# Filling TensorE's waits in the routing stage, and moving two experts' down weights to the end of the load queue

## The reference

```python
h = h + merged @ w_out
u2 = rmsnorm(h, norm_ffn)
p_group = softmax(u2 @ wg + bg)                    # 4 groups, the best one is taken
e_logits = (u2 @ we + be)[chosen group]            # 8 experts in it, the best two are taken
combine = one_hot(group) * g_val * weights_of_the_two
for each of the 32 experts e:                      # 1024 -> 256 -> 1024
    y += (silu(u2 @ w_gate[e]) * (u2 @ w_up[e]) * combine[e]) @ w_down[e]
out = rmsnorm(h + y, norm_final)
```

## Time and profile before

| | us |
|---|---|
| Median of 3 runs | 1137.32 (1136.3 to 1138.05) |
| The profiled execution's own time | 1138.34 |
| Its span, first to last instruction | 1136.5 |
| PE busy in the span | 1040.1 (92%) |
| DVE, ACT, POOL busy | 476.9, 314.8, 59.0 |
| DMA, mean over the span | 153 GB/s |

### The profile page before, as it was taken

How to read it: one execution, slowest core, us unless ns; L and a number is a source line. 1 busy time by engine, 2 the same in 40 slices (tenths; PEclk the granted TensorE clock), 3 DMA queues, 4 the chain that set the end, 5 groups by cost and what they waited for, 6 DMA issues and landing times.

```text
span 1136.5 us, 15499 instructions
## 1 busy us (share of the span) xinstructions
PE 1040.1 (92%) x6445; PEld 630.8 (55%) x6445; DVE 476.9 (42%) x972; ACT 314.8 (28%) x602; POOL 59.0 (5%) x69
## 2 busy tenths in 40 slices
PE   6999999998999999999999999999996999787780
PEld 6665656675575575575566566444454655344440
DVE  4536364637337337337335454523235321111115
ACT  3535344434234334334332122110110111100112
POOL 1000000000000000000000000000001222211110
PEclk9999999999999999999999999999996999988995
DMA  9322222233132132132112111044936999999945
GB/s 287 90 64 66 57 57 56 56 80 73 39 63 72 38 65 70 39 65 70 38 37 75 56 56 57 1 160 165 366 143 240 408 414 416 416 418 414 418 200 231
DMA packets 111946, 174.41 MB, mean 153 GB/s; under 512 B 9012, under 2 KB 87101, under 8 KB 103555
## 3 DMA queue, kind: packets, MB, share of 16 engines
q1 hardware_dynamic: 97890, 130.73, 33.3%
q10 hardware_dynamic: 8256, 31.53, 7.0%
q0 software_dynamic: 5728, 11.14, 3.9%
HBM read 169.16 MB, written 12.60 MB: 160 GB/s over the span
## 4 chain that ended last, share of the span: by engine, by line
PE 68%; DMA 14%; DVE 12%; ACT 3%; issue 2%; SPq 1%; POOL 0%; DVEq 0%; POOLq 0%
PE ps L746 21%; DMA arena<-in_expert_w_up 11%; PE ps L737 7%; PE ps L743 7%; PE ps L744 6%; PE ps L2001 6%; DVE arena L1284 4%; PE ps L1707 3%; PE ps L791 3%; PE ps L2008 2%; PE ps L770 1%; DVE arena L1441 1%; DVE yT L2330 1%; DVE arena L1520 1%; DVE arena L1517 1%
## 5 line engine op out<-in xcount | busy, mean ns | idle before, releaser
L746 PE MATMUL ps<-arena 128*128 128x512 f32 x672 | 314.0, 602 | 0.0
L746 PEld LDWEIGHTS ps<-arena 128*128 128x128 f32 x672 | 119.6, 190 | 113.6 <-issue 108.5
L2001 PE MATMUL ps<-arena,gates 128*64 128x256 f32 x864 | 107.7, 406 | 25.9 <-DMA arena<-in_expert_w_up 24.4
L743 PE MATMUL ps<-arena 128*128 128x264 f32 x416 | 127.9, 389 | 0.8 <-DVE gates L1356 0.8
L744 PE MATMUL ps<-arena 128*128 128x264 f32 x416 | 126.6, 386 | 0.0
L1284 DVE TENSOR_TENSOR arena<-arena 128x256 f32<-128x256 f32 (+6 forms) x194 | 91.5, 516 | 56.5 <-ACT arena L1105 34.3
L2001 PEld LDWEIGHTS ps<-arena,gates 128*64 128x64 f32 x864 | 65.0, 147 | 75.4 <-DMA arena<-in_expert_w_up 35.0
L737 PE MATMUL ps<-yT,arena 128*128 128x512 f32 x192 | 84.8, 596 | 2.2 <-DVE gates L1356 1.4
L744 PEld LDWEIGHTS ps<-arena 128*128 128x128 f32 x416 | 79.0, 190 | 13.5
L743 PEld LDWEIGHTS ps<-arena 128*128 128x128 f32 x416 | 76.0, 190 | 16.3 <-issue 4.7
L2156 DVE COPY gates<-ps 128x1024 f32<-128x1024 f32 x16 | 19.6, 1225 | 110.7 <-PE ps L1988 110.7
(11 more groups left out here) (329 smaller groups left out, 1257.8 us busy)
## 6 DMA issues: line engine op xcount, KB each, us to landing
arena<-in_w_in SPq DMA_DIRECT2D x68, 512.0 KB, 3.8
arena<-in_expert_w_gate SPq DMA_DIRECT2D x27, 1024.0 KB, 28.9
arena<-in_expert_w_up SPq DMA_DIRECT2D x27, 1024.0 KB, 34.6
arena<-in_expert_w_down ACTq DMA_DIRECT2D x18, 1024.0 KB, 32.7
arena<-in_w_branch SPq DMA_DIRECT2D x12, 512.0 KB, 3.9
C<-in_expert_w_gate SPq DMA_DIRECT2D x5, 1024.0 KB, 32.3
gates<-in_expert_w_up SPq DMA_DIRECT2D x5, 1024.0 KB, 38.5
arena<-in_w_out SPq DMA_DIRECT2D x1, 4096.0 KB, 13.8
```

Of the source, the lines that this page charges most:

```text
L743: t.matmul(dst[:, 0:HALF], wt, uT[:, k, 0:HALF], start=(k == 0), stop=(k == KD - 1))
L746: mm = t.matmul(dst, wt, uT[:, k, META:], start=(k == 0), stop=(k == KD - 1))
L2001: mm = t.matmul(dst, toks[:, k, :], src, start=(k == 0), stop=(k == KD - 1))
```

## The change

It has four parts.

1. **Repeated product.** PE gets a function `keep_busy(n)` that makes n products of the identity matrix with 512 columns of the transposed tokens into PSUM bank 5; nobody reads them. It stands 15 times behind the last logits, 2 times behind "ct" and 11 times behind "tb".
2. **Last tile.** The logits of tiles 0 to 2 are scaled ahead of the last copy of the last tile (PE signals them with a new step "l2"), those of tile 3 in one step "l3" from a bank of their own. The last tile is normed ahead of "l3", not behind "num", and ACT stores it ahead of its two exponentials.
3. **Shorter chain.** "O1" and "O2" become one step "O", for which "og" is made twice as wide, and "dm" moves behind "num".
4. **Down weights.** `LATE = 2`: the down weights of experts 30 and 31 are no longer issued by ACT but by SP, behind the last gate and up weights.

```diff
             rows_order = [..., "t2", "u2", "t3a", "h7",
-                          "t3b"]
+                          "sc", "lb", "t3b", "u3"]
...
 scalar:
+                a.wait_ge(*dve2.after(f"u{NT - 1}"))
+                a.dma_start(u2_dram[(NT - 1) * P:, :], u2[:, NT - 1, :]).then_inc(sem("rows_kept"), 16)
                 a.wait_ge(*dve2.after("lt"))
                 a.activation(gx, lt, ACT.Exp).then_inc(*act2.did("eg"))
                 a.wait_ge(*dve2.after("dm"))
                 a.activation(e2, dm, ACT.Exp).then_inc(*act2.did("e2"))
-                a.wait_ge(*dve2.after(f"u{NT - 1}"))
-                a.dma_start(u2_dram[(NT - 1) * P:, :], u2[:, NT - 1, :]).then_inc(sem("rows_kept"), 16)
...
 tensor:
+                def keep_busy(n):
+                    for _ in range(n):
+                        t.matmul(bank(5), ident, u2T[:, KD - 1, :], start=True, stop=True)
...
-                logits(2, every, "t2")
+                logits(2, every, "t2").then_inc(*pe2.did("l2"))
                 turn_tokens(3, high_half, "T3b")
                 logits(3, low_half, "t3a")
                 logits(3, high_half, "t3b").then_inc(*pe2.did("lg"))
+                keep_busy(15)
                 t.wait_ge(*dve2.after("M"))
...
                 mm.then_inc(*pe2.did("ct"))
+                keep_busy(2)
...
                 mm.then_inc(*pe2.did("tb"))
+                keep_busy(11)
...
 vector:
+                first = NT - 1
+                v.wait_ge(*pe2.after("l2"))
+                tt("sc", lg[:, 0:first, :], bank(0, first * 36)..., ss2[:, 0:first]..., ALU.mult)
+                tt("lb", lg[:, 0:first, :], lg[:, 0:first, :], over(rb, first), ALU.add)
                 turned(NT - 1, 1)
+                normed(NT - 1)
                 v.wait_ge(*pe2.after("lg"))
-                v.wait_ge(*act2.after(f"rs{NT - 1}"))
-                tt("sc", lg, bank(0, NT * 36)..., ss2..., ALU.mult)
-                tt("lb", lg, lg, over(rb, NT), ALU.add)
+                step("l3", v.scalar_tensor_tensor(lg[:, first, :], logit_bank(first), ss2[:, first:NT], rb, ALU.mult, ALU.add))
...
-                tt("dm", dm, m2, m1, ALU.subtract)
-                for k, o_ in ((0, o1), (1, o2)):
-                    tt(f"O{k + 1}", chosen[:, k, :]..., og..., o_..., ALU.mult)
+                tt("O", chosen..., og..., o12..., ALU.mult)
                 tt("M", mm_, chosen[:, 0, :], chosen[:, 1, :], ALU.add)
                 tt("num", numbered, by_expert, NUM..., ALU.mult)
-                normed(NT - 1)
+                tt("dm", dm, m2, m1, ALU.subtract)
...
 esync:
                 for e in range(NX - U):
                     sp.wait_ge(*up_made.of(e))
                     load_up(sp, e % U, e + U)
+                for e in range(NX - U - LATE, NX - U):
+                    sp.wait_ge(*made.of(e))
+                    load_down(sp, e % U, e + U)
...
 escalar:
-                    if e + U < NX:
+                    if e + U < NX - LATE:
                         load_down(a, e % U, e + U)
```

More of the change, by code:

```diff
@@ L1622, in tail @@
             nfin = gates[:, 22:24, :].rearrange("p a t -> p (a t)")
-            pe2 = Steps(sem("router_pe"), ["o0", "o1", "o2", "T0", "o3", "o4", "T1", "o5", "o6", "T2", "T3a", "o7", "T3b", "lg",
+            pe2 = Steps(sem("router_pe"), ["o0", "o1", "o2", "T0", "o3", "o4", "T1", "o5", "o6", "T2", "T3a", "o7", "l2", "T3b", "lg",
                                            "rk", "ct", "tb"])
-            choose = ["sc", "lb", "gm", "lt", "gd", "gx", "og", "el", "es", "m1", "e1", "q1", "x1", "o1",
-                      "n2", "m2", "e2", "q2", "x2", "o2", "dm", "O1", "O2", "M", "num", f"u{NT - 1}"]
+            choose = ["l3", "gm", "lt", "gd", "gx", "og", "el", "es", "m1", "e1", "q1", "x1", "o1",
+                      "n2", "m2", "e2", "q2", "x2", "o2", "O", "M", "num", "dm"]
             place = ["rk", "pos", "sl0", "sl1", "vi", "xe", "xo", "yi"]
@@ L1630, in tail @@
                     ["sx", "jb", "jc"], ["jd", "ji", "ni", "eq", "en", "et"], ["vx", "xx", "yx"]]
-            rows_order = ["wn", "h0", "h1", "h2", "t0", "u0", "h3", "h4", "t1", "u1", "h5", "h6", "t2", "u2", "t3a", "h7", "t3b"]
+            rows_order = ["wn", "h0", "h1", "h2", "t0", "u0", "h3", "h4", "t1", "u1", "h5", "h6", "t2", "u2", "t3a", "h7", "sc", "lb", "t3b", "u3"]
             dve2 = Steps(sem("router_dve"), rows_order + choose + place + share + [n for part in more for n in part])
@@ L1681, in scalar, with logit_bank @@
                 a.activation(e2, dm, ACT.Exp).then_inc(*act2.did("e2"))
-                a.wait_ge(*dve2.after(f"u{NT - 1}"))
-                a.dma_start(u2_dram[(NT - 1) * P:, :], u2[:, NT - 1, :]).then_inc(sem("rows_kept"), 16)
+            def logit_bank(i):
+                return bank(0)[:, i * 36:(i + 1) * 36] if i < NT - 1 else bank(1, 36)
             def tensor(t):
@@ L1697, in logits @@
                     for k in ks:
-                        mm = t.matmul(bank(0)[:, i * 36:(i + 1) * 36], u2T[:, k, i * P:(i + 1) * P], wr[:, k, :],
+                        mm = t.matmul(logit_bank(i), u2T[:, k, i * P:(i + 1) * P], wr[:, k, :],
                                       start=(k == 0), stop=(k == KD - 1))
@@ L1746, in tensor @@
                 mm.then_inc(*pe2.did("tb"))
-            lt, gx, og = small(NT, NG), small(NT, NG), small(NT, NG)
+                keep_busy(11)
+            lt, gx, og = small(NT, NG), small(NT, NG), small(2 * NT, NG)
             t4 = small(NT, NG)
             gm, gv, m1, m2, dm, e2, mx = (small(NT) for _ in range(7))
-            el, o1, o2, t8 = small(NT, NE), small(NT, NE), small(NT, NE), small(NT, NE)
+            el, t8, o12 = small(NT, NE), small(NT, NE), small(2 * NT, NE)
+            o1, o2 = o12[:, 0:NT, :], o12[:, NT:, :]
             chosen = small(2, NT * NX)
@@ L1830, in vector @@
                     residual(2 * i + 1)
+                step, tt, ts, red, slots_of = small_steps(v)
+                first = NT - 1
+                v.wait_ge(*pe2.after("l2"))
+                tt("sc", lg[:, 0:first, :], bank(0, first * 36).rearrange("p (i c) -> p i c", i=first),
+                   ss2[:, 0:first].unsqueeze(2).broadcast_to([P, first, 36]), ALU.mult)
+                tt("lb", lg[:, 0:first, :], lg[:, 0:first, :], over(rb, first), ALU.add)
                 turned(NT - 1, 1)
-                step, tt, ts, red, slots_of = small_steps(v)
+                normed(NT - 1)
                 def wide(ap, n):
@@ L1837, in vector @@
                 v.wait_ge(*pe2.after("lg"))
-                v.wait_ge(*act2.after(f"rs{NT - 1}"))
-                tt("sc", lg, bank(0, NT * 36).rearrange("p (i c) -> p i c", i=NT), ss2.unsqueeze(2).broadcast_to([P, NT, 36]), ALU.mult)
-                tt("lb", lg, lg, over(rb, NT), ALU.add)
+                step("l3", v.scalar_tensor_tensor(lg[:, first, :], logit_bank(first), ss2[:, first:NT], rb, ALU.mult, ALU.add))
                 g4, g32 = lg[:, :, 0:NG], lg[:, :, NG:].rearrange("p i (g e) -> p i g e", g=NG)
@@ L1846, in vector @@
                 red("gx", mx, t4, ALU.max)
-                tt("og", og, t4, wide(mx, NG), ALU.is_equal)
-                tt("el", sel, g32, og.unsqueeze(3).broadcast_to([P, NT, NG, NE]), ALU.mult)
+                tt("og", og.rearrange("p (k i) g -> p k i g", k=2), t4.unsqueeze(1).broadcast_to([P, 2, NT, NG]),
+                   mx.unsqueeze(1).unsqueeze(3).broadcast_to([P, 2, NT, NG]), ALU.is_equal)
+                tt("el", sel, g32, og[:, 0:NT, :].unsqueeze(3).broadcast_to([P, NT, NG, NE]), ALU.mult)
                 red("es", el, sel.rearrange("p i g e -> p i e g"), ALU.add)
@@ L1859, in vector @@
                     tt("o" + n, o_, t8, wide(mx, NE), ALU.is_equal)
-                tt("dm", dm, m2, m1, ALU.subtract)
-                for k, o_ in ((0, o1), (1, o2)):
-                    tt(f"O{k + 1}", chosen[:, k, :].rearrange("p (i g e) -> p i g e", i=NT, g=NG),
-                       og.unsqueeze(3).broadcast_to([P, NT, NG, NE]), o_.unsqueeze(2).broadcast_to([P, NT, NG, NE]), ALU.mult)
+                tt("O", chosen.rearrange("p k (i g e) -> p (k i) g e", i=NT, g=NG), og.unsqueeze(3).broadcast_to([P, 2 * NT, NG, NE]),
+                   o12.unsqueeze(2).broadcast_to([P, 2 * NT, NG, NE]), ALU.mult)
                 tt("M", mm_, chosen[:, 0, :], chosen[:, 1, :], ALU.add)
                 tt("num", numbered, by_expert, NUM.unsqueeze(2).broadcast_to([P, 2 * NT, NX]), ALU.mult)
-                normed(NT - 1)
+                tt("dm", dm, m2, m1, ALU.subtract)
                 v.wait_ge(*pe2.after("rk"))
@@ L1896, in tail @@
             WX, WP, PAIR = 3 * 2 * D, 2 * D, 2 * SLOTS
-            U, YR = 6, len(yr)
+            U, YR, LATE = 6, len(yr), 2
             def in_one(at):
```

## The result

The changed kernel took 1143.29 us at the median of 5 runs (1141.23 to 1144.25), beside 1137.32 for the kernel before (5 runs, 1136.3 to 1140.33) in the same comparison. The medians are 6.0 us apart. The ratio, which is formed from all the runs and not from the two medians, is 1.0042, 95% interval 1.0029 to 1.0055: slower by 0.42%, about 4.8 us. The profiled execution took 1141.74, 3.4 more than the 1138.34 of the one profiled before, with a span of 1139.8.

What follows compares the result with a forecast made beforehand. Transfers were taken to bound the expert stage, at 416 GB/s. Its shift of +7.7 us and -5.7 at the end made +2.0: 1140.3 us for the profiled execution, 1139.3 for the median, range 1131 to 1142.5.

Steps and rivals of the forecast that it cites:

- The filler's price: PE, routing stage: 0.86 us per repeated product, so 12.9, 1.7 and 9.4 us in waits of 6.15, about 0.7 and 5.12.
- Rival 3: Routing stage: a repeated product costs half, 0.43 us, and the fillers fit; 9.3 us less, 1128.0 us; chance 0.10.
- The steps of the routing stage: From the last logits to up(0): each step dated behind the fillers, first transposes done at 877.8 against 868.75, 9.05 us late.
- The shift of the expert stage: Expert stage: its transfers start later by 9.05 - 1.3 = 7.7 us, bounds 7.3 and 8.3.
- the hole of 1.3: DMA engines at 876 to 878 us: a gap between the first released loads that closes, worth 1.3 us.
- rival 4: Expert stage: six sets of buffers absorb the late release, only the -5.7 us is left, 1131.6 us; chance 0.08.
- the gain of 5.7 us: End of the expert stage: with two down loads moved, up(30) and up(31) start without a wait; PE ends 5.7 us earlier.
- rival 1: End of the expert stage: moving the last two down loads gives nothing back, only +7.7 us is left, 1145 us; chance 0.10.
- Rival 2: End of the expert stage: up(31) still waits and starts cold, gain 3.4 us for 5.7, 1141.6 us; chance 0.12.
- The sum: Whole kernel: +7.7 us for the expert stage's shift and -5.7 at the end make +2.0 us.
- within 0.2%: Whole kernel: difference under 2.3 us, not to be told from none; called the likeliest case, chance 0.38.
- slower: Whole kernel: the changed kernel is slower by more than 0.2% (2.3 us); chance 0.42.

Runs made afterwards that it cites:

- Half the width: The changed kernel with each repeated product cut from 512 to 256 columns, counts 15, 2 and 11 kept: 1130.57 us, ratio 0.9941 to the kernel before.
- filler alone: The kernel before with the 15, 2 and 11 repeated products and nothing else: 1145.39 us, ratio 1.0063.
- with chain: The changed kernel with LATE = 0, so ACT issues all down weights as before; filler and shortened chain stay: 1146.11 us, ratio 1.0067 to the kernel before.
- moved loads alone: The kernel before with only the last two experts' down weights issued by SP behind the last gate and up weights: 1134.65 us, ratio 0.9965.
- no filler: The changed kernel without any repeated product; shortened chain and moved down weights stay: 1133.99 us, ratio 0.9955 to the kernel before.
- the chain alone: The kernel before with only the changes to the last tile and to DVE's chain: 1137.23 us, ratio 0.9993.
- two, three and four moved loads: The changed kernel with 6, 1 and 5 repeated products and LATE = 2, 3, 4: 1130.54, 1127.12, 1129.62 us; ratios to the kernel before 0.9933, 0.9902, 0.9922.
- the longer third group: The changed kernel with 16 instead of 11 repeated products in the third group: 1145.52 us, ratio 1.0069 to the kernel before.

## Why the prediction was right or wrong

**The filler's price was right.** 0.86 us for a product was forecast from the two instructions to a product in the earlier trace rows. The three groups took 12.96, 1.9 and 9.5 us to the start of what stood behind them; 12.9, 1.7 and 9.4 were forecast. Half the width on the same counts brought the time below that of before, which excludes a price by instruction. Rival 3, half the price, is excluded by the 56 instructions and the 13.12 us of the first group.

**The steps of the routing stage were right.** On the old axis (0.37 taken off), forecast and measured: ranking from 863.0, 863.0; table read at 867.5, 867.8; first transposes begin at 876.7, 877.2; they are done at 877.8, 878.2; up(0) done at 882.9, 883.3. DVE's shorter chain was hidden behind the filler, as forecast (filler alone 1.0063, with chain 1.0067).

**The shift of the expert stage was right.** 7.7 us was forecast (9.05 less the hole of 1.3). Up(29) came 7.6 later in the profile, and the runs gave +7.6 and +7.2 for the filler with and without the chain. That it fits so well is in part luck: the first transposes were done 9.5 us late, not 9.05, and what came off between there and up(29) was 1.9 us, not the 1.3 of the hole. Five further products, worth 4.3 us, added 4.3 to R and took nothing off X, so in the traces the six sets of buffers absorb nothing (rival 4 falls).

**The step that failed is a term at the end**, the gain of 5.7 us. It rests on "so up(30) starts there, without a wait", from down weights of experts 30 and 31 that would compete with expert 30's gate and up weights. In the pairs of kernels that differ in the two moved loads only, X fell by 4.0 (moved loads alone), 4.3 (no filler, beside the chain alone) and 4.0 to 4.2 (the changed kernel's two profiles, beside the one without moved loads); the runs of the moved loads alone gave 4.0. In the same pairs E fell by 4.8 to 5.2, but in the kernels without filler up(29) started 1.0 us later, for a reason that I have not found. Up(30) still waited 0.66 to 1.50 us. Its weights landed 7.4 to 8.3 us behind those of expert 29, 8.1 before, where 6.5 was forecast. I had let the two loads take part in the sharing from the start, but on ACT's queue they stood behind expert 29's down load. The kernel before shows it. This is that load (buffer gates), from the rows of its down weights between 1055.6 and 1056.4 us:

```profile
L1943 ACTq DMA_DIRECT2D gates<-in_expert_w_down x1: 374/374/374, 1055.9 to 1055.9; - x1
DMA to landing us min/median/max: 31.5/31.5/31.5
```

It landed at 1055.9 + 31.5 = 1087.4, only 0.5 us ahead of up(30)'s start at 1087.93. Expert 28's down load, issued at 1042.9, had landed 36.7 us later, at 1079.6, when up(29)'s weights came. So what passed between the two starts was 3 MiB, the down weights of expert 29 and the gate and up weights of expert 30; by my estimate from 416 GB/s that takes 7.6 us, and nearly nothing is left for the loads that were moved. Moving expert 29's down load too took the wait away (E 21.8), as this account says.

That the end gives nothing back (rival 1) is excluded by the moved loads alone. Rival 2, a cold start of up(31), was not seen in any profile with two moved loads: the low clock fell on up(29) instead in the changed kernel (and in the one with half the width), where it took the place of up(30)'s wait (E 23.3, beside 22.7 to 23.5 in the other profiles with two moved loads).

**The sum.** With 4.7 for 5.7 it is +2.9 to +3.0, and the two profiled executions of the changed kernel are 3.4 and 3.3 above the one of before. The runs say more: by ratios +4.8 and, the second time, +6.3, by medians +6.0 and +5.2, where the parts measured apart add up to +7.6 - 4.0 = +3.6 (+3.3 by medians). The intervals (1.4 to 1.8 us each way for each ratio) overlap, so the parts may well add. **Open** is whether typical runs hold 1.4 to 3 us that neither profile of the changed kernel has. A fall of the clock at the head of the first filler would fit in size, 1.7 us; it is in five of the eight other profiles of kernels with a filler. The mean granted clock of whole executions points the same way, but weakly: the two fastest of the changed kernel's eleven (1141.23 and 1141.62 us) had 0.987 and 0.989 and the slowest (1147.75) had 0.975, yet one of 1141.74 had 0.979. No profile shows a slower run of this kernel, so this is a candidate, not a finding.

My forecast of 1139.3 was too low by 4.0 us against the median of 1143.29, which lies 0.8 above the range that I gave (up to 1142.5); by the ratio, 1.0042 on 1137.32, the time is 1142.1, just inside it. I had called "within 0.2%" the likeliest case, though my chances had a little more on "slower" (0.42 beside 0.38), since the sum of +2.0 us ended at the bound of 2.3. Slower came, for the mechanism that I had named; that it came clear of that bound is owed to the gain at the end, which I had too large, and to the part that is open, and so it is luck in part.

## What to carry to other kernels

Work put into a wait to keep an engine warm must be sized in that engine's own instructions, from the trace, and end before the wait does; what it runs over is paid if something behind it releases the next stage. Read what a stage's end releases, not how busy it is: here PE at 100% and the high clock was the slower version, and half as much filler the faster one. When loads are to give way to others at the end of a stream, look at what is ahead of them in their own queue first, then move as many as take the last wait away and no more: two, three and four moved loads gave 0.9933, 0.9902 and 0.9922 (the intervals of the last two overlap a little; X was 233.4, 232.0 and 232.2).

## What the runs showed of the hardware

- **The clock can fall while PE is busy.** In the profiles of five kernels the granted clock was at 0.50 for some 3 us in the first filler, though PE had had no idle time of more than 0.3 us in the 40 us ahead of it; just before it stand transposes and the logits products with 36 columns. Below is the kernel with the longer third group: PE busy 3.00 of 3.00 at a clock of 0.50. In the other five profiles with a filler it stayed at 1.00 there. In the first filler of 15 it costs 1.7 us.

```profile
846.00:850.00 4.00, 3.89 (x33) 3.68 (x33) 2.92 (x6) 1.65 (x4) 0.00 (x0) 0.99 0.77 281
850.00:853.00 3.00, 3.00 (x5) 1.09 (x4) 2.58 (x13) 0.22 (x1) 0.00 (x0) 0.50 1.00 371
853.00:856.00 3.00, 3.00 (x8) 1.40 (x7) 2.44 (x10) 0.19 (x1) 0.00 (x0) 0.95 1.00 358
```

- **It falls at about the same place without a filler.** In all four profiles without one the clock fell 0.5 to 0.8 us behind the end of the last logits, when nearly the whole wait for M was still to come. So it did not take a wait of several us there either. In the kernel before PE's logits ended at 850.0 us:

```profile
850.00:851.00 1.00, 0.03 (x1) 0.00 (x0) 0.83 (x4) 0.00 (x0) 0.00 (x0) 0.82 0.94 393
851.00:852.00 1.00, 0.00 (x0) 0.00 (x0) 0.86 (x5) 0.22 (x1) 0.00 (x0) 0.50 1.02 434
```

- The Trainium skill, "TensorE: Matmul & The Clock Gate", section "Why this matters for your kernels", asks to leave no idle gaps between bursts of matmuls. The trace agrees that the clock is low in such gaps (0.50 from 856 to 862), but here it also fell with gaps of 0.3 us at most, after small products: leaving no gap was not enough. A filler that fitted did keep the clock at 1.00 from its first group to the first transposes in the kernel with half the width.
- **Low-clock starts cost little where the next transfer is late anyway**: in experts 27 to 29 up products of 5.0 to 6.5 us instead of 3.7 came and went between executions, while X stayed at 233.4 to 233.8 with two moved loads and a filler, and at 237.8 with a filler and none moved.
